# The modulation row moved from a TensorE stage at the start into VectorE's time inside the two feed-forwards

## The chip, the cores and the metric

The kernel runs on one core of a Trainium2 chip. The metric is the device time of one execution in microseconds (us), the median of several runs.

## The reference, cut to what matters

A stream `x` of 256 tokens by 1024 runs through two blocks in float32. The first has a retention mixer, a feed-forward, a gated linear recurrence and a second feed-forward. The second block scales and shifts its normed input by a modulation row, mixes with a context of 256 tokens, and ends in a product-key feed-forward. The modulation row depends on nothing that the first block computes:

```python
def swiglu_ffn(x, w_in, w_out):
    gate, up = jnp.split(x @ w_in, 2, axis=-1)
    return (jax.nn.silu(gate) * up) @ w_out
...
mod_l = jax.nn.silu(c) @ ada_w[i] + ada_b[i]          # c: (1, 1024), ada_w: (1024, 6144)
mod_c = jax.nn.silu(c_ctx) @ ada_w[i] + ada_b[i]
sh1, sc1, g1, sh2, sc2, g2 = jnp.split(mod_l[:, None, :], 6, axis=-1)
csh1, csc1, cg1, csh2, csc2, cg2 = jnp.split(mod_c, 6, axis=-1)
hl = rmsnorm(xl, norm1_g[i]) * (1.0 + sc1) + sh1
hc = rmsnorm(xc, norm1_g[i]) * (1.0 + csc1) + csh1
yc, yl = token_mixing(hc, hl, ...)
xl = xl + g1 * yl
hl2 = rmsnorm(xl, norm2_g[i]) * (1.0 + sc2) + sh2
xl = xl + g2 * peer_ffn(hl2, ...)
```

Of `mod_c` only the first two sixths (`csh1`, `csc1`) are used. `ada_w` is 25 MB.

## The kernel before, in words

Every large product is made of three TensorE products. A weight slot of 128 x 4096 float32 (2 MB; `wraw`, two buffers) is loaded by SyncE's queue, ScalarE copies it into a high part (`split_hi`, L934, four pieces), VectorE subtracts to get a low part (`split_lo`, L1300, four pieces), and TensorE multiplies high by high, low by high and high by low (`mm3`, L1831 to L1833). A slot's buffer is loaded again once VectorE has split it (`s_wlo`), and its split parts are overwritten once TensorE has used them (`s_wused`). PSUM banks 0 to 3 are handed round by `unit`, `take` and `free_bank`; banks 4 to 7 are an accumulator. Each engine runs its own program in a fixed order, written out by hand, and a waiting instruction holds all behind it on its engine.

**The start.** SyncE loads constants and the small parameter rows (`prow`), and then twelve slots of `ada_w`, with `x` after the fourth. TensorE turns the parameter rows into columns; ScalarE takes the silu of `c` and `c_ctx`, and through Abs, Exp and Ln (L974 to L978) with eleven small VectorE instructions (L1382 to L1394) makes a column that the recurrence needs. In `ada` each of the twelve slots is split and multiplied, 24 products of 512 columns a slot; VectorE adds the bias (L1403), and GpSimd stores 512 columns of the modulation row to DRAM (`mods`), from where they are later read back broadcast into `rows`. Then come norm 0 (squares L947, root L951, gain L1334, TensorE transposes L1893, high part L955, low part L1326), the retention input (twelve slots) and the retention heads. A head needs a masked score (L1433) ahead of its products with the values (L1971 to L1975).

**A feed-forward** has eleven "in" steps (a 2 MB slot; 96 products of 256 columns) and eleven "out" steps (a 1 MB slot; 24 products of 512 columns), in the order in 0, in 1, out 0, in 2, out 1, ..., in 10, out 9, out 10. In its step each engine splits the slot of the next step. After an "in" step VectorE multiplies gate by up (`ffn_hidden`, L1468) and GpSimd splits it (L813, L814). The middle sixteen steps are four trips of a hardware loop of four steps, with semaphore targets and addresses computed from the trip. During the second feed-forward the context is loaded, normed, modulated and transposed too (`norm_c`).

**The input of the recurrence** is a hardware loop of three trips; in each VectorE runs a four-tap convolution (L1488 to L1497) on one bank after another, every instruction waiting for the one before it.

## Time and profile before

| | |
|---|---|
| median of 3 runs | 2549.86 us (2546.12 to 2551.75) |
| the profiled execution, its own time | 2535.93 us |
| its span | 2534.1 us |
| TensorE matmul, busy | 2255.3 us (89%) |
| VectorE, busy | 1426.4 us (56%) |
| ScalarE, busy | 1061.1 us (42%) |
| GpSimd, busy | 294.2 us (12%) |
| read from HBM | 333.71 MB, 132 GB/s over the span |

In the rows below PE is TensorE's matmuls and PEld its weight loads, DVE VectorE, ACT ScalarE, POOL GpSimd, SPq SyncE's queue. L12 is line 12 of the kernel; many helpers are shared, so a line can serve several stages. The busy time of a stretch tells how full an engine was; the timeline's bracket tells how long the engine stood idle ahead of an instruction and what released it. "x4" merges instructions that follow each other, and their time is from the first start to the last end. A float32 product that is not split in parts shows as two matmul records.

### The profile page before, as it was taken

The page shows a single profiled execution, that of the slowest core. Times are in us where ns is not written, and L with a number is a line of the kernel's source. Part 1 is how long each engine was busy: PE and PEld are TensorE (multiplying, and loading weights), DVE is VectorE, ACT ScalarE, POOL GpSimd, SP SyncE. Part 2 cuts the span into 40 slices and gives each one's busy share as a digit, 9 for nine tenths or more (in the row PEclk, how much of TensorE's full clock was granted, in tenths as well). Part 3 has the DMA queues.
Part 4 walks back from the last instruction along what each step waited for, and adds up shares of the span by engine and source line. Part 5 has one row for each costly group of instructions (what it writes and reads, how often), then busy time and mean ns, then how long its engine had stood idle before and what let it go on. Part 6 is the DMA issues. An engine that isn't in the chain of part 4 may idle for free.

```text
span 2534.1 us, 38849 instructions
## 1 busy us (share of the span) xinstructions
PE 2255.3 (89%) x14663; PEld 2014.7 (80%) x14663; DVE 1426.4 (56%) x2220; ACT 1061.1 (42%) x1872; POOL 294.2 (12%) x307
## 2 busy tenths in 40 slices
PE   5799989979768997988998887989999999999997
PEld 4587678869758886977887467889999999877775
DVE  5753554466765455215445334699666663566665
ACT  4535343344553433313332243433444444555554
POOL 1120111111211120000003000000123342000000
PEclk9899999999879998988998588999999999999998
DMA  8845335453334445230010022334333334666664
GB/s 319 289 170 193 109 122 177 166 182 125 125 121 145 149 149 183 92 110 1 1 25 10 1 91 92 118 117 134 109 117 113 114 117 145 188 189 187 189 190 140
DMA packets 158604, 336.58 MB, mean 133 GB/s; under 512 B 17818, under 2 KB 69776, under 8 KB 158352
## 3 DMA queue, kind: packets, MB, share of 16 engines
q1 hardware_dynamic: 153872, 321.15, 39.4%
q0 software_dynamic: 4608, 13.68, 1.6%
q8 instruction: 88, 1.44, 0.2%
q14 instruction: 36, 0.29, 0.0%
HBM read 333.71 MB, written 1.10 MB: 132 GB/s over the span
## 4 chain that ended last, share of the span: by engine, by line
PE 54%; DVE 16%; PEld 15%; issue 5%; ACT 3%; DMA 3%; PEldq 2%; POOL 0%; SPq 0%; DVEq 0%; ACTq 0%
PE psum L1831 12%; PE psum L1833 12%; PE psum L1832 12%; PEld psum L1831 5%; PEld psum L1832 5%; PEld psum L1833 5%; DVE weights_lo L1300 5%; PE psum L2304 4%; PE psum L2351 2%; PEldq L1878 2%; ACT weights_hi L934 2%; PE psum L2168 2%; PE psum L2174 2%; DMA weights<-in_ada_w_dram 1%; DVE u_lo L1781 1%
## 5 line engine op out<-in xcount | busy, mean ns | idle before, releaser
L1300 DVE TENSOR_TENSOR weights_lo<-weights,weights_hi 128x1024 fp32r<-128x1024 f32 (+2 forms) x384 | 446.4, 1225 | 217.2 <-ACT weights_hi L934 215.7
L934 ACT ACTIVATE weights_hi<-weights 128x1024 fp32r<-128x1024 f32 (+2 forms) x384 | 335.0, 945 | 281.7 <-PEq L1878 161.6
L1831 PE MATMUL psum<-input_hi,weights_hi 128*128 128x256 f32 x1288 | 373.0, 290 | 46.4 <-DVE weights_lo L1300 32.4
L1832 PE MATMUL psum<-input_lo,weights_hi 128*128 128x256 f32 x1288 | 369.3, 287 | 0.0
L1833 PE MATMUL psum<-input_hi,weights_lo 128*128 128x256 f32 x1288 | 368.8, 286 | 0.0
L1831 PE MATMUL psum<-input_hi,u_hi 128*128 128x256 f32 x1024 | 301.5, 294 | 0.0
L1831 PEld LDWEIGHTS psum<-input_hi,weights_hi 128*128 128x128 f32 x1288 | 251.9, 196 | 58.2 <-issue 33.0
L1832 PE MATMUL psum<-input_lo,u_hi 128*128 128x256 f32 x1024 | 290.6, 284 | 0.0
L1833 PE MATMUL psum<-input_hi,u_lo 128*128 128x256 f32 x1024 | 290.5, 284 | 0.0
L1781 DVE TENSOR_TENSOR u_lo<-psum,u_hi 128x512 fp32r<-128x512 f32 x256 | 164.9, 685 | 178.5 <-ACT u_hi L1231 177.3
L1833 PEld LDWEIGHTS psum<-input_hi,weights_lo 128*128 128x128 f32 x1288 | 252.1, 196 | 0.0
L1832 PEld LDWEIGHTS psum<-input_lo,weights_hi 128*128 128x128 f32 x1288 | 252.0, 196 | 0.0
L1831 PE MATMUL psum<-v_hi,act_hi 128*128 128x512 f32 x512 | 203.4, 397 | 0.0
L1833 PE MATMUL psum<-v_hi,act_lo 128*128 128x512 f32 x512 | 200.4, 391 | 0.0
L1832 PE MATMUL psum<-v_lo,act_hi 128*128 128x512 f32 x512 | 200.0, 391 | 0.0
L1832 PEld LDWEIGHTS psum<-input_lo,u_hi 128*128 128x128 f32 x1024 | 197.6, 193 | 0.0
L1831 PEld LDWEIGHTS psum<-input_hi,u_hi 128*128 128x128 f32 x1024 | 197.0, 192 | 0.0
L1833 PEld LDWEIGHTS psum<-input_hi,u_lo 128*128 128x128 f32 x1024 | 196.9, 192 | 0.0
L1231 ACT ACTIVATE u_hi<-psum 128x512 fp32r<-128x512 f32 x256 | 139.4, 597 | 42.1 <-PE psum L2304 35.8
L2304 PE MATMUL psum<-ident,u_rows 128*128 128x128 f32 x1024 | 135.9, 276 | 17.4 <-DVE u_lo L1781 16.4
L2304 PEld LDWEIGHTS psum<-ident,u_rows 128*128 128x128 f32 x1024 | 116.1, 142 | 21.6 <-issue 19.8
L1808 DVE TENSOR_TENSOR act_lo<-act_table,act_hi 128x256 fp32r<-128x256 f32 x128 | 54.7, 428 | 136.9 <-ACT act_hi L1277 136.9
(367 smaller groups left out, 4217.8 us busy)
## 6 DMA issues: line engine op xcount, KB each, us to landing
u_rows<-in_peer_u_dram SPq DMA_DIRECT2D x128, 512.0 KB, 3.6
weights<-in_ffn_w_in_dram SPq DMA_DIRECT2D x44, 1024.0 KB, 6.5
v_rows_even<-in_peer_v_dram SPq DMA_DIRECT2D x64, 512.0 KB, 3.6
v_rows_odd<-in_peer_v_dram SPq DMA_DIRECT2D x64, 512.0 KB, 3.6
weights<-in_ada_w_dram SPq DMA_DIRECT2D x24, 1024.0 KB, 7.5
weights<-in_ret_w_in_dram SPq DMA_DIRECT2D x24, 1024.0 KB, 6.4
weights<-in_ffn_w_out_dram SPq DMA_DIRECT2D x44, 512.0 KB, 7.1
weights<-in_lru_w_in_dram SPq DMA_DIRECT2D x12, 1024.0 KB, 6.7
```

The lines of the kernel that those rows point to most:

```text
L934: nc.scalar.activation(whi[:, r, at_], wraw[:, r, at_], ACT.Copy).then_inc(s_whi[r], 1)
L1231: nc.scalar.activation(UTH[:, b, 4 * h:4 * h + 4, :], PS[:, h, :].rearrange("p (k e) -> p k e", k=4), ACT.Copy).then_inc(s_uh[b], 1)
L1300: ins = nc.vector.tensor_tensor(wlo[:, r, at_], wraw[:, r, at_], whi[:, r, at_].bitcast(F32), ALU.subtract)
L1781: nc.vector.tensor_tensor(UTL[:, b, 4 * h:4 * h + 4, :], PS[:, h, :].rearrange("p (k e) -> p k e", k=4), UTH[:, b, 4 * h:4 * h + 4, :].bit ...
L1808: nc.vector.tensor_tensor(AL[:, b:b + 1, :], GT[:, bass.ds(4 * i + j, 1), :], AH[:, b:b + 1, :].bitcast(F32), ALU.subtract).then_inc(s_as, 1)
L1831: nc.tensor.matmul(o, ah, bh, start=start, stop=False)
L1832: nc.tensor.matmul(o, ah, bl, start=False, stop=False)
L1833: return nc.tensor.matmul(o, al, bh, start=False, stop=stop)
L1878: pe.drain().then_inc(s_wused[r], 1)
L2168: ins = nc.tensor.matmul(quarter(j), AM[d][:, j // 2, j % 2, :], XX[d][:, j // 2, j % 2, :], start=True, stop=True)
L2174: ins = nc.tensor.matmul(quarter(j), TI[d][:, j // 2, j % 2, :], YY[d][:, j // 2, j % 2, :], start=True, stop=True)
L2304: ins = nc.tensor.transpose(PS[:, h, q * P:(q + 1) * P], UR[:, b, at_:at_ + P], ident[:, :])
```

## The change

The `ada` stage at the start goes. Its sum is made on VectorE as 128 fused multiply-adds of 128 x 512 (`ada_product`): each takes a block of 128 rows of `ada_w`, unsplit, times a column of silu(c) or silu(c_ctx), plus the running sum. Twelve blocks of 512 columns are made: 0 to 5 in the first feed-forward, 80 products, eight in each of steps 1, 3, ..., 19; 6 to 11 in the second, 48 products, six in each of steps 5, 7, ..., 19. They stand behind `split_lo` and ahead of the `ffn_hidden` product of an "in" step. In the step after a block's last product TensorE adds up the 128 partitions by a float32 product with a column block of ones (two products for blocks 0 to 3, one for the others), ScalarE copies the result and GpSimd stores it.

The 24 halves of `ada_w` (1 MB each) have two buffers of their own, `AW`, beside the feed-forward's. SyncE loads them between the feed-forward's slots, each behind a wait (`s_awused`) for the half that lay there before. The first two wait for the end of the mixer ahead (`s_acc`), whose tiles lie there. The bias is loaded into partition 0 of a zeroed tile.

At the start `x`, the identity and two retention slots are loaded first, the parameter rows next, and norm 0 comes first on all engines. The Abs, Exp, Ln chain and its VectorE instructions stand between the retention input and the heads. All hardware loops of these stages are written out. The readers of `mods` wait for the stores (`stored`). `IOTA` shares `prow`'s place.

```diff
+FFN_STEPS = [("in", 0)]
+for _n in range(FI - 1):
+    FFN_STEPS += [("in", _n + 1), ("out", _n)]
+FFN_STEPS += [("out", FI - 1)]
+ADA_SLOTS = {"ffn0": range(0, 6), "ffn1": range(6, 12)}
+ADA_FIRST = {"ffn0": 1, "ffn1": 5}
+ADA_STEP = {"ffn0": 8, "ffn1": 6}
+BOTH = 4
+def ada_products(name):
+    return [(q, k, m) for q in ADA_SLOTS[name] for k in range(KT) for m in range(2 if q < BOTH else 1)]
+def ada_step(name, n):
+    return ADA_FIRST[name] + 2 * (n // ADA_STEP[name])
+def ada_made(name, at_):
+    return [p for n, p in enumerate(ada_products(name)) if ada_step(name, n) == at_]
+def ada_summed(name, at_):
+    last = {p[0]: ada_step(name, n) for n, p in enumerate(ada_products(name))}
+    return [q for q in ADA_SLOTS[name] if last[q] + 1 == at_]
+def ada_loaded(name, at_):
+    halves = [(q, h) for q in ADA_SLOTS[name] for h in range(2)]
+    last = {(p[0], p[1] // 4): ada_step(name, n) for n, p in enumerate(ada_products(name))}
+    return [half for n, half in enumerate(halves)
+            if (ADA_LOAD[name] if n < 2 else last[halves[n - 2]] + 2) == at_]
+ADA_LOAD = {"ffn0": 1, "ffn1": 2}
...
 SyncE
-            ada(0)
-            sp.dma_start(X[:, :, :], ...).then_inc(s_xload, 16)
-            with sp.Fori(1, 3) as i:
-                ada(i)
+            sp.dma_start(X[:, :, :], ...).then_inc(s_xload, 16)
+            sp.dma_start(ident[:, :], cols("ident")).then_inc(s_ident, 16)
+            for j in range(2):
+                wide(SLOTS["ret_in"] + j, W["ret_w_in"], j * BANK)
...
+            def load_ada(q, h):
+                if 2 * q + h >= 2:
+                    sp.wait_ge(s_awused, 2 * q + h - 1)
+                if h == 0:
+                    sp.wait_ge(s_azero, 1)
+                    sp.dma_start(AB[0:1, q % 4, :], A["ada_b_2"][0:1, q * BANK:(q + 1) * BANK]).then_inc(s_ab[q % 4], 16)
+                sp.dma_start(AW[:, h, :, :], W["ada_w_2"][:, 4 * h:4 * h + 4, q * BANK:(q + 1) * BANK])\
+                    .then_inc(s_aw[h], 16)
...
+                def load_context(at_):
+                    if at_ == ADA_LOAD[name]:
+                        sp.wait_ge(s_acc, 2 if name == "ffn0" else 6)
+                    for q, h in ada_loaded(name, at_):
+                        load_ada(q, h)
+                    if name == "ffn1" and at_ == 2:
+                        sp.dma_start(XC[:, :, :], ...).then_inc(s_ctx, 16)
...
 GpSimd
+                    for q in ada_summed(name, at_):
+                        evacuated(ada_unit(q))
+                        for half in range(2 if q < BOTH else 1):
+                            pool.dma_start(mods[half:half + 1, q * BANK:(q + 1) * BANK],
+                                           astage[64 * half:64 * half + 1, q % 2, :]).then_inc(s_ast[q % 2], 16)
...
 ScalarE
-            rounds(act, 3, ada)
             norm(0)
+            split_hi(0)
...
+                    for q in ada_summed(name, at_):
+                        b = take(ada_unit(q))
...
+                        nc.scalar.activation(astage[rows_, q % 2, :], PS[rows_, b, :], ACT.Copy).then_inc(s_free[b], 1)
...
 VectorE
+            def ada_product(q, k, m):
+                if (k, m) == (0, 0):
+                    dve.wait_ge(s_csilu, 1)
+                    dve.wait_ge(s_ab[q % 4], 16 * (q // 4 + 1))
...
+                chain.done(nc.vector.scalar_tensor_tensor(
+                    total, AW[:, k // 4, k % 4, :], csilu[:, 8 * m + k:8 * m + k + 1],
+                    total if k else AB[:, q % 4, :], ALU.mult, ALU.add))
...
+                def step(kind, n, at_):
+                    split_lo(sbase + at_ + 1, n=after(at_, last))
+                    for q, k, m in ada_made(name, at_):
+                        ada_product(q, k, m)
                     if kind == "in":
...
 TensorE
-            rounds(pe, 3, ada)
+                    for q in ada_summed(name, at_):
+                        b = free_bank(ada_unit(q))
...
+                        pe.wait_ge(s_asum, q + 1)
+                        for m in range(2 if q < BOTH else 1):
+                            ins = nc.tensor.matmul(PS[64 * m:64 * m + 64, b, :], ones[:, :], AS[m][:, q % 2, :],
+                                                   start=True, stop=True)
```

## Rows read from the trace of the kernel before

**Rows 1.** Busy time by stretch: start:end, length, each engine's time (instructions), TensorE clock, DMA share, GB/s

```profile
0.00:115.60 115.60, 75.66 (x289) 57.13 (x289) 74.03 (x85) 59.27 (x66) 20.07 (x44) 0.96 0.90 317
346.00:551.00 205.00, 186.77 (x1296) 171.56 (x1296) 99.88 (x95) 70.07 (x96) 34.08 (x22) 1.00 0.46 154
```

**Rows 2.** Chain of waits that ended last, first 130 us: start, length, what

```profile
51.22 11.05 DMA weights<-in_ada_w_dram
...
120.77 0.38 PE psum L1831
```

**Rows 3.** Busy time of two short stretches of the start, same columns as the first group

```profile
2.00:4.00 2.00, 0.00 (x0) 0.00 (x0) 0.00 (x0) 0.03 (x1) 2.00 (x4) 1.00 0.47 179
14.00:17.00 3.00, 0.00 (x0) 0.00 (x0) 1.13 (x7) 0.00 (x0) 0.00 (x0) 1.00 1.05 389
```

**Rows 4.** Timeline, first norm: start, length, engine, line, out<-in, count, idle before and its releaser

```profile
111.25 1.04 ACT L947 ACTIVATE normed<-residual 128x1024 f32<-128x1024 f32 x1
...
119.02 0.60 ACT L955 ACTIVATE input_hi<-psum 128x512 fp32r<-128x512 f32 x1 [0.26 <-PE psum L1893]
...
120.67 4.63 DVE L1300 TENSOR_TENSOR weights_lo<-weights,weights_hi 128x1024 fp32r<-128x1024 f32 x4 [0.32 <-ACT weights_hi L934]
```

**Rows 5.** Timeline, all engines, first 30 us

```profile
9.77 0.20 ACT L974 ACTIVATE small<-param_cols 128x12 f32<-128x12 f32 x1
...
15.16 0.17 DVE L1394 TENSOR_SCALAR small<-small 128x12 f32<-128x12 f32 x1
...
26.36 0.63 PE L1832 MATMUL psum<-weights_lo,c_hi 128*128 128x512 f32 x1
...
28.23 0.39 PE L1832 MATMUL psum<-weights_lo,c_hi 128*128 128x512 f32 x1
```

**Rows 6.** Timeline, all engines, one pair of feed-forward steps

```profile
408.90 0.69 DVE L1468 TENSOR_TENSOR ffn_hidden<-psum,ffn_gate 128x512 f32<-128x512 f32 x1 [9.55 <-PE psum L1833]
...
410.01 8.77 DVE L1300 TENSOR_TENSOR weights_lo<-weights,weights_hi 128x1024 fp32r<-128x1024 f32 x8 [0.42 <-ACT weights_hi L934]
...
410.87 2.15 POOL L814 TENSOR_TENSOR ffn_lo<-ffn_hidden,ffn_hi 128x512 fp32r<-128x512 f32 x1
...
414.96 2.19 ACT L934 ACTIVATE weights_hi<-weights 128x512 fp32r<-128x512 f32 x4 [2.13 <-PE psum L1833]
...
416.51 0.38 PE L1831 MATMUL psum<-input_hi,weights_hi 128*128 128x256 f32 x1 [1.65 <-DVE weights_lo L1300]
416.54 1.01 SPq L686 DMA_DIRECT2D weights<-in_ffn_w_in_dram  x2
...
418.95 0.89 SPq L686 DMA_DIRECT2D weights<-in_ffn_w_out_dram  x2
...
428.40 0.69 DVE L1468 TENSOR_TENSOR ffn_hidden<-psum,ffn_gate 128x512 f32<-128x512 f32 x1 [9.62 <-PE psum L1833]
```

**Rows 7.** Groups of instructions, VectorE, whole span, shapes apart: count, busy, mean ns, idle before

```profile
L1497 DVE SCALAR_TENSOR_TENSOR lru_u<-lru_padded,param_cols,lru_u 128x256 f32 x36 | 17.4, 485 | 5.4 <-DVE lru_u L1497 1.8 <-DVE lru_u L1495 1.8
...
L1512 DVE SCALAR_TENSOR_TENSOR lru_q<-lru_q,lru_r 128x512 f32<-128x512 f32 x6 | 4.2, 692 | 0.2
```

**Rows 8.** DMA to landing of the weight loads issued at 416.5 and at 419

```profile
DMA to landing us min/median/max: 5.2/6.4/7.6
...
DMA to landing us min/median/max: 7.1/7.4/7.8
```

**Rows 9.** Timeline, VectorE, first trip of the recurrent block's input loop

```profile
590.77 0.41 DVE L1495 TENSOR_SCALAR lru_u<-lru_padded,param_cols 128x256 f32 x1 [0.44 <-DVE lru_padded L1488]
...
593.43 0.41 DVE L1495 TENSOR_SCALAR lru_u<-lru_padded,param_cols 128x256 f32 x1 [0.32 <-DVE lru_u L1497]
...
603.51 10.77 DVE L1300 TENSOR_TENSOR weights_lo<-weights,weights_hi 128x1024 fp32r<-128x1024 f32 x8 [0.53 <-DVE lru_u L1497]
```

**Rows 10.** Timeline, ScalarE and VectorE, first retention head

```profile
262.50 0.60 ACT L998 ACTIVATE gate_silu<-psum 128x512 f32 x1 [4.84 <-PE psum L1833]
...
264.44 0.56 DVE L1433 TENSOR_TENSOR scores<-psum,decay 128x384 f32<-128x384 f32 x1 [7.16 <-PE psum L1961]
```

**Rows 11.** Chain of waits that ended last, retention heads

```profile
266.58 0.86 PE psum L1974 x2
```

**Rows 12.** Timeline, ScalarE and TensorE, end of the first feed-forward

```profile
551.08 3.90 ACT L934 ACTIVATE weights_hi<-weights 128x1024 fp32r<-128x1024 f32 x4 [3.72 <-PE psum L1833]
...
551.28 0.47 PE L1831 MATMUL psum<-weights_hi,ffn_hi 128*128 128x512 f32 x1 [0.30 <-PE psum L1833]
```

More of the change, by code:

```diff
@@ L191, in slot, with ffn_steps, ffn_unit, ada_unit @@
     return s0 % 2, i * (per // 2) + s0 // 2
-FFN_HEAD = [("in", 0), ("in", 1), ("out", 0)]
-FFN_BODY = [("in", 2), ("out", 1), ("in", 3), ("out", 2)]
-FFN_TAIL = [("in", FI - 1), ("out", FI - 2), ("out", FI - 1)]
-FFN_TRIPS = (FI - 3) // 2
-FFN_BASE = {"ffn0": 0, "ffn1": FI}
-FFN_SIZE = {"in": SLOT, "out": 2 * D}
-def ffn_steps(eng, base, step, chain=None, per=0, early=None, late=None):
-    for k, (kind, n) in enumerate(FFN_HEAD):
-        step(kind, n, base + k)
-    if early:
-        early()
-    with eng.Fori(0, FFN_TRIPS) as i:
-        if chain:
-            chain.enter(i, per)
-        for k, (kind, n) in enumerate(FFN_BODY):
-            step(kind, n, base + len(FFN_HEAD) + k, i)
-    if chain:
-        chain.leave(FFN_TRIPS)
-    if late:
-        late()
-    for k, (kind, n) in enumerate(FFN_TAIL):
-        step(kind, n, base + 2 * FI - len(FFN_TAIL) + k)
-def rounds(eng, trips, body):
-    body(0)
-    with eng.Fori(1, trips) as i:
-        body(i)
-def ffn_unit(name, n):
-    return UNITS[name] + 2 * n + (4 if name == "ffn1" and n >= 2 else 0)
-def after(base, s0, last):
-    order = FFN_HEAD + FFN_BODY * FFN_TRIPS + FFN_TAIL
-    n = s0 - base + 1
-    return FFN_SIZE[order[n][0]] if n < len(order) else last
+def ffn_steps(step, beside=None):
+    for at_, (kind, n) in enumerate(FFN_STEPS):
+        step(kind, n, at_)
+        if beside:
+            beside(at_)
+def ffn_unit(name, n, half=0):
+    return UNITS[name] + FFN_UNITS[name].index(("in", 2 * n + half))
+def ada_unit(q):
+    name = "ffn0" if q in ADA_SLOTS["ffn0"] else "ffn1"
+    return UNITS[name] + FFN_UNITS[name].index(("ada", q))
+def after(at_, last):
+    return FFN_SIZE[FFN_STEPS[at_ + 1][0]] if at_ + 1 < len(FFN_STEPS) else last
 NA_STEPS = TT * 8
@@ L422, in first_and_second_block @@
         split_at = stage.at
+        beside_ffn = Region("beside the feed-forward", stage_at + 16 * KB, split_at - stage_at - 16 * KB)
+        AW = beside_ffn.take("ada_rows_in", [P, 2, 4, BANK])
+        AS = [beside_ffn.take("ada_sums", [P, 2, BANK]),
+              Region("context, before it", split_at, 4 * KB).take("ada_sums_c", [P, 2, BANK])]
+        astage = beside_ffn.take("ada_rows", [P, 2, BANK])
         CH = stage.take("context_hi", [P, KT, S], F32R)
@@ L501, in first_and_second_block @@
         HKT = low.take("picks_t", [P, 3, S])
-        IOTA = low.take("iota", [P, P])
+        IOTA = prow
         GE = low.take("gates", [P, 2, 4, P])
@@ L1036, in _ @@
             norm(2)
-            with act.Fori(0, 3) as i:
+            for i in range(3):
                 for j in range(2):
@@ L1369, in _ @@
             nc.vector.memset(eps_col, EPS).then_inc(s_eps, 1)
+            nc.vector.memset(ones[:, :], 1.0).then_inc(s_ones, 1)
+            norm(0)
+            split_lo(0)
             b = take(UNITS["param"])
@@ L1471, in step, with beside @@
                         dve.sem_inc(s_free[b], 1)
[L1473 removed]
+                def beside(at_):
+                    if name == "ffn1" and at_ == 2:
+                        modulated("norm_c", XC, CH, CL)
+                ffn_steps(step, beside)
             norm(1)
@@ L1479, in _ @@
             chain.done(nc.vector.memset(UP[:, :, 0:3], 0.0))
-            with dve.Fori(0, 3) as i:
-                chain.enter(i, 2 * 9)
+            for i in range(3):
                 for j in range(2):
@@ L1500, in _ @@
                         dve.sem_inc(s_uc, 1)
-            chain.leave(3)
             split_lo(SLOTS["lru_gate"] + 1, n=3072)
@@ L1944, in _ @@
                     used(r)
-            with pe.Fori(0, 4) as i:
+            for i in range(4):
                 for j in range(2):
@@ L2015, in _ @@
             transposes(2)
-            with pe.Fori(0, 3) as i:
+            for i in range(3):
                 for j in range(2):
```

281 lines of the change are left out of this document (133 added, 148 removed).

## The prediction

> **What bounds the kernel now.** I read the busy times by stretch first. The first 115.6 us are a stage that DMA sets: the 16 DMA engines are busy 0.90 of it at 317 GB/s, while TensorE is busy 75.66 us [rows 1]. The chain of waits says the same: its long links there are weight slots of the modulation matrix on their way, one of 11.05 us, and the retention input's first product starts only at 120.77 us [rows 2]. The feed-forwards are another kind of stage: in 346 to 551 us TensorE is busy 186.77 of 205 us, VectorE only 99.88 us, and DMA 0.46 of its time [rows 1]. So I read the timeline of one pair of steps there, to see where VectorE, SyncE's queue and DMA have room and which wait ends last. The pair's period is 428.40 - 408.90 = 19.5 us [rows 6]. The chain in it is: "in" products end, ScalarE's first high piece, four low pieces on VectorE, next "in" products. TensorE does the "out" step meanwhile and then stands for 1.65 us, until VectorE's low parts at 416.51 [rows 6].
>
> **The front.** The 25 MB leave the start. What then sets the first retention product? `x` (1.05 MB) shares DMA with GpSimd's three gain rows (1.57 MB). Traffic is at 179 GB/s in 2 to 4 us and at 389 GB/s once full [rows 3]; half filled, 2.1 MB take some 6 us from 2.5 us on, so I put `x` at 8.5 us (estimate; 6 to 11 as bounds). From the first square (111.25) to the end of ScalarE's last high copy (119.02 + 0.60) are 8.4 us, then ScalarE turns to the slot's high parts: 16.9 us, plus 1 us for transposes on a slow TensorE, 17.9. The low parts start 1.05 us after such a turn (120.67 against 119.62) and take 4.63 us [rows 4]. That gives 23.6 us. The data come sooner: `x`, gain rows, identity and the first slot are 4.8 MB, 12.4 us at 389 GB/s from some 3.5 us on; the parameter rows, which TensorE now waits for behind both slots, are at 6.9 MB, some 22 us. I take 23.6 where 120.77 stood: **-97.2 us**. Here the old stage hid a cost: its first matmuls took 0.63 us each and those after 27.2 us 0.39 us [rows 5], 4 us at about half speed under a DMA wait. Now that falls on the retention input, which TensorE sets: half of 4 us, **+2**. The twelve slots of 2.1 MB need 5.4 us each at 389 GB/s and TensorE takes some 12, so DMA doesn't bind there.
>
> **The heads.** The Abs to last small VectorE instruction took 9.77 to 15.33 us, 5.6 us, with two table loads inside [rows 5]. At the start it hid behind the first slot's loading. Its new place is behind the last gate copy, which ends at 262.50 + 0.60 = 263.10; so it ends at 268.7, and VectorE's first masked score, at 264.44 before, is queued behind it [rows 10]: 4.3 us. TensorE's products with the values wait for that score. After such a pause it may be slow again for a few products; nothing shows it here, 0 to 2 us, and I take 0.7 because the float32 products there are short: **+5**.
>
> **The recurrence's input.** Written out, the loop loses its computed targets and addresses. In a trip VectorE stands 0.44 and 0.32 us ahead of each first tap, both kinds twice, and 0.53 ahead of the next split [rows 9], 2.05 us; where nothing new is computed the same wait for the instruction before is 5.4/36 = 0.15 us [rows 7]. Five times 0.15 are 0.75, so 1.3 us a trip could go, and VectorE is in the chain there: three trips, 3.9. I take **-3.7**; bounds 0 and -5.
>
> **The products inside the feed-forwards.** A product is 692 ns, a fused multiply-add of the same 128 x 512, plus 0.15 us for its wait: 0.85 us, eight are 6.8 us [rows 7]. VectorE has finished both splits at 410.01 + 8.77 = 418.78, so products end at 425.6, and the gate product comes at 428.40 when TensorE is done [rows 6]. 2.8 us are left, and they cover the work entirely. If the cover went, each microsecond past 428.4 would cost one in each of the 18 pairs with products. All 128 products are 109 us of VectorE, at nothing on the path. In a pair that ends a block ScalarE's high parts of the "out" slot (414.96) now queue behind TensorE's one or two products with ones and a copy of 0.6 us. A float32 product of 512 columns is 0.86 us [rows 11], so two and the copy push those high parts 2.5 us and the low parts, which had slack in front of them, some 1.8; products then end at 427.4, still ahead.
>
> TensorE: two products are 1.7 us in a gap of 1.65 and start a little late, 0.3 us for each of blocks 0 to 3, and nothing for the eight with one product: +1.2. At the end of each feed-forward there's no gap: out 10 follows out 9 by 0.30 us at 551.28, and ScalarE's next high parts at 551.08 lie on the chain into the norm [rows 12]. One product, the copy and their hand-overs stand ahead, 1.8 us, twice: +3.6. The trips' boundaries and computed waits go: the pairs should lose 0.1 us, sixteen of them, -1.6 (bounds 0 and -4). Sum **+3.2**.
>
> SyncE's queue is the tight place. A load of the next half waits there for the half's products, at 425.6, and behind it waits the "out" slot, which was issued at 418.95. Together they are 2 MB, like the "in" pair, whose last landed 7.6 us after its own issue, half a microsecond behind the first [rows 6, 8]: some 8 us. So the "out" slot lands at 433.6 where ScalarE wants it at 414.96 + 19.5 = 434.5. It is a loop of its own: landing 8, first high piece 0.6, low parts 2.7, products 6.8, hand-overs 0.3, together 18.4 against 19.5. After a block's end it is late by about 1 us, which the 2.8 us take up. The "in" slot is issued before the wait, at 416.54, and isn't touched. GpSimd's stores, half a microsecond each to issue, fall where it idles, and the readers of the row come far later.
>
> VectorE and GpSimd: the eight splits take 8.77 us where alone they'd be 4.63 + 2.7; the surplus falls beside GpSimd's work of 410.87 to 413.02 [rows 4, 6]. The products run at 418.8 to 425.6, clear of it. The Trainium skill (GPSIMD Engine Reference, Specifications) says that GpSimd's SBUF interface is shared with VectorE, with contention when a VectorE instruction has two SBUF inputs, as each of these products has. The splits beside GpSimd agree. By that rule the products would be slowed if the two met; on this timetable they don't, and the sum would be the same.
>
> **Sum.** -97.2 + 2 + 5 - 3.7 + 3.2 = -90.7, on the profiled execution's 2535.9: 2445. The runs' median is 2549.86, 14 us above that execution; I carry the difference over: 2549.9 - 90.7 = **2459 us**.
>
> **Rivals.**
> - *SyncE's loop binds.* If half and "out" slot land after 11 us, not 8 (one slot of the first stage took 11.05 [rows 2]), the loop is 21.4 us and some 18 pairs lose 1.9 each: +34, 2493. Against it: DMA here is busy under half the time. Chance 0.15.
> - *Products meet GpSimd.* The splits went from 7.3 to 8.8 us beside 2 to 3 us of its work [rows 6], a slowdown of 1.3 if all is charged to four splits of 4.63. Eight products at 1.3 times 0.85 are 8.9 us and end at 427.7, still covered; but the loop is 20.5, 1.0 over, in the ten pairs of the first feed-forward (six products stay under in the second): +10, 2469. The skill's rule named above speaks for it, the order in time against. Chance 0.06.
> - *The front comes later.* `x` at 11 us, a cold TensorE through both the transposes and the first slot, parameter rows that arrive last: +8, 2467. Nothing in the old trace shows `x` alone. Chance 0.14.
> - *More is gained*: written-out waits save 0.3 us a pair and `x` lands at 6: -8, 2451. Chance 0.07.
> - *Slower than before.* One mechanism: the "out" slot, held in SyncE's queue behind `s_awused`, comes so late that it drags every pair. It decides from 4.5 us a pair, 91/20, so at a landing of some 14 us instead of 8; at 15 the loop is 25.4 us and costs 5.9 in 20 pairs, 118, which gives 2577. Nothing shows such a landing for 2 MB at half load. Chance 0.02.
> - *It doesn't do what it says*: the start stays as long, because loads of the retention slots take the matrix's place as the bound, 2550. They'd have to come at under a third of the measured rate. Chance 0.01.
>
> The likeliest holds 0.55. What a measurement here can't tell from no change is about 0.2%, 5 us.
>
> **Range and chances.** The likeliest, the late front, the larger gain and the products beside GpSimd hold 0.82 and lie at 2451 to 2469; with 8 us below and 13 above for their own bounds (the loops' 0 instead of -3.7, the pause's 2 us, the spread of 6 us among three runs) I take 2443 to 2482. Faster 0.97, same 0.01, slower 0.02.
>
> **What would show it.** The first retention product at 22 to 26 us, and its first ones at half speed. The first masked score 5.6 us behind the last gate copy. Feed-forward pairs of 19.4 to 19.8 us, VectorE's products between 418.8 and 425.6 of such a pair with over 2 us idle behind them, each 0.69 us and 0.85 apart. The "out" slot's high parts still released by TensorE and not by a DMA. Wrong if the high parts wait for the "out" slot's DMA, if the gate product waits for the products, or if the front ends past 32 us.

## The result, and the profile after

The kernel after takes **2436.6 us** (median of 6 runs, 2411.5 to 2441.8) where the one before takes 2550.2 (6 runs, 2546.1 to 2556.4): ratio 0.9552, 95% interval 0.951 to 0.9594. The forecast was 2459 us in 2443 to 2482. The sign was right and the gain bigger: 113.6 us between the medians, 90.7 forecast, and the time lies 6.4 us below the range. The profiled execution of after took 2429.3 us with a span of 2427.5, 106.6 under that of before.

To see where they went I cut both traces at the same marks, VectorE's products of `ffn_hidden` (L1468 before, L1521 after; eleven in each feed-forward). Lengths in us:

| | before | after | difference | forecast |
|---|---|---|---|---|
| start to the first product of feed-forward 0 | 358.02 | 264.58 | -93.4 | -90.2 |
| first to last product of feed-forward 0 | 187.03 | 185.39 | -1.6 | +0.4 |
| its last product to the first of feed-forward 1 | 219.77 | 212.67 | **-7.1** | -1.9 |
| first to last product of feed-forward 1 | 199.93 | 196.03 | **-3.9** | -0.8 |
| its last product to the end | 1569.35 | 1568.83 | -0.5 | +1.8 |

(The forecast's terms laid on these stretches: -97.2 + 2 + 5; +1.2 of the products with ones and half of the -1.6; +1.8 - 3.7; the other half of the -1.6; +1.8. A feed-forward's stretch holds one step of 12.0 us and nine pairs.) The stretches in bold are those that came out too well. Each length is from one execution; the same stretch of kernels that don't differ in it moves by some 2 to 3 us from one execution to the next (the front of before 357.9 to 360.4, the third stretch of after 211.1 to 213.5), so single differences of 1 or 2 us say little.

**The front.** Timeline of after, all engines, the rows that answer to [rows 4]: start, length, engine, line, out<-in, count, idle before and what ended it.

```profile
6.01 1.28 ACT L994 ACT_TABLE_LOAD   x1 [6.01 <-DMA residual<-in_x_dram]
...
16.26 3.90 ACT L981 ACTIVATE weights_hi<-weights 128x1024 fp32r<-128x1024 f32 x4 [0.22 <-DMA weights<-in_ret_w_in_dram]
17.34 4.63 DVE L1350 TENSOR_TENSOR weights_lo<-weights,weights_hi 128x1024 fp32r<-128x1024 f32 x4 [0.58 <-ACT weights_hi L981]
...
23.50 0.43 PE L1974 MATMUL psum<-ident,param_rows 118*128 118x118 f32 x1 [8.09 <-DMA param_rows<-in_sc_conv_w_dram]
23.63 0.55 PE L1880 MATMUL psum<-input_hi,weights_hi 128*128 128x256 f32 x1
...
28.67 0.41 PE L1882 MATMUL psum<-input_hi,weights_lo 128*128 128x256 f32 x1
...
29.68 0.28 PE L1882 MATMUL psum<-input_hi,weights_lo 128*128 128x256 f32 x1
```

The first retention product stands at 23.63, the forecast to 0.03 us, but not by the forecast's chain: the low parts are done at 17.34 + 4.63 = 21.97, 1.6 us sooner than I had them, and the parameter rows, put at "some 22", end TensorE's wait at 23.50. That the two errors meet so closely is luck. `x` was there at 6.01, not at 8.5. The products take 0.41 us until 29.1 and 0.28 from then on.

**The heads.** Timeline of after, the rows that answer to [rows 10].

```profile
165.21 0.60 ACT L1031 ACTIVATE gate_silu<-psum 128x512 f32<-128x512 f32 x1 [4.84 <-PE psum L1882]
...
165.93 1.28 ACT L1035 ACT_TABLE_LOAD   x1
...
171.11 0.17 DVE L1460 TENSOR_SCALAR small<-small 128x12 f32<-128x12 f32 x1
171.19 1.01 DVE L1465 TENSOR_TENSOR scores<-psum,decay 128x384 f32<-128x384 f32 x2
171.99 1.37 PE L2007 MATMUL psum<-values,scores 128*128 128x512 f32 x2 [3.70 <-DVE scores L1465]
```

The first masked score is 5.4 us behind the last gate copy (171.19 - 165.81), and TensorE stood 3.70 us for it. Busy time by stretch after that pause (start:end, length, each engine's time, TensorE clock, DMA share, GB/s) shows a mean granted clock of 0.67 of the full 2.4 GHz, so a part of it at the lower level, 1.2 GHz:

```profile
171.90:177.00 5.10, 5.01 (x10) 2.42 (x11) 1.64 (x4) 0.00 (x0) 0.00 (x0) 0.67 0.00 0
```

**A pair of feed-forward steps.** Timeline of after, answering to [rows 6].

```profile
315.12 0.69 DVE L1521 TENSOR_TENSOR ffn_hidden<-psum,ffn_gate 128x512 f32<-128x512 f32 x1 [2.10 <-PE psum L1882]
316.61 8.32 DVE L1350 TENSOR_TENSOR weights_lo<-weights,weights_hi 128x1024 fp32r<-128x1024 f32 x8 [0.79 <-ACT weights_hi L981]
321.44 2.19 ACT L981 ACTIVATE weights_hi<-weights 128x512 fp32r<-128x512 f32 x4 [2.02 <-DMA weights<-in_ffn_w_out_dram]
322.58 0.39 PE L1880 MATMUL psum<-input_hi,weights_hi 128*128 128x256 f32 x1 [1.52 <-DVE weights_lo L1350]
324.86 0.74 DVE L1498 SCALAR_TENSOR_TENSOR ada_sums<-ada_rows_in,small,ada_sums 128x512 f32<-128x512 f32 x1
...
330.35 0.75 DVE L1498 SCALAR_TENSOR_TENSOR ada_sums_c<-ada_rows_in,small,ada_sums_c 128x512 f32<-128x512 f32 x1
331.19 0.37 SPq L712 DMA_DIRECT2D ada_rows_in<-in_ada_w_dram  x1
331.60 0.98 SPq L726 DMA_DIRECT2D weights<-in_ffn_w_out_dram  x2
334.38 0.69 DVE L1521 TENSOR_TENSOR ffn_hidden<-psum,ffn_gate 128x512 f32<-128x512 f32 x1 [3.27 <-PE psum L1882]
```

The pair is 19.26 us long, and all nine of the first feed-forward are 19.26 or 19.27. The eight products start 0.785 us apart ((330.35 - 324.86) / 7), end at 331.1, and 3.27 us are left behind them; in pairs that end a block 2.10 (the first row). One thing that I had named as a sign of a wrong forecast is there: in this pair the high parts of the "out" slot wait for its DMA, 2.02 us. VectorE's eight splits run through without a gap all the same, so nobody waits for them.

DMA issues of the next half and "out" slot (KB each, median us from issue to landing):

```profile
ada_rows_in<-in_ada_w_dram SPq DMA_DIRECT2D x1, 1024.0 KB, 5.3
weights<-in_ffn_w_out_dram SPq DMA_DIRECT2D x2, 512.0 KB, 6.5
```

**The recurrence's input.** Timeline of after, VectorE and then ScalarE, one trip of what was the loop, answering to [rows 9].

```profile
497.00 0.41 DVE L1550 TENSOR_SCALAR lru_u<-lru_padded,param_cols 128x256 f32<-128x256 f32 x1 [0.16 <-DVE lru_padded L1543]
497.44 1.53 DVE L1552 SCALAR_TENSOR_TENSOR lru_u<-lru_padded,param_cols,lru_u 128x256 f32<-128x256 f32 x3
...
502.01 3.90 ACT L981 ACTIVATE weights_hi<-weights 128x1024 fp32r<-128x1024 f32 x4 [7.73 <-PEq L1927]
...
526.02 3.90 ACT L981 ACTIVATE weights_hi<-weights 128x1024 fp32r<-128x1024 f32 x4 [7.72 <-PEq L1927]
```

From one trip's high parts to the next one's are 526.02 - 502.01 = 24.01 us. Before, ScalarE's rows for the same places are these (timeline, ScalarE):

```profile
595.48 1.28 ACT L934 ACT_TABLE_LOAD   x1 [7.60 <-PEq L1878]
596.78 3.90 ACT L934 ACTIVATE weights_hi<-weights 128x1024 fp32r<-128x1024 f32 x4
602.21 1.28 ACT L1043 ACT_TABLE_LOAD   x1 [1.53 <-PE psum L1833]
...
624.47 3.90 ACT L934 ACTIVATE weights_hi<-weights 128x1024 fp32r<-128x1024 f32 x4
```

There it was 624.47 - 596.78 = 27.69 us: 3.7 us more a trip, where I had costed 1.3. (The loop has two such full turns; behind its last copy of a bank VectorE saves 2.3 us more.) Two things differ. In the loop ScalarE loads its activation table twice in each trip, which I had not looked at, and VectorE waits ahead of each instruction. The Trainium skill (ScalarE activation tables: per-element evaluation and per-set limits, Table sets in the compiler and the runtime) says that the back end places the table loads per block. A loop's body that is such a block would load at each trip, as this one does, 1.28 us each.

**The end of a feed-forward.** Timeline of after, ScalarE, answering to [rows 12].

```profile
457.28 0.59 ACT L1074 ACTIVATE ada_rows<-psum 64x512 f32<-64x512 f32 x1 [5.01 <-PE psum L2054]
457.77 3.89 ACT L981 ACTIVATE weights_hi<-weights 128x1024 fp32r<-128x1024 f32 x4
461.57 1.01 ACT L994 ACTIVATE normed<-psum 128x1024 f32<-128x1024 f32 x1
```

The squares that open the norm start 461.57 - 449.97 = 11.60 us behind the last `ffn_hidden` product. Before (timeline, ScalarE) they stood 554.89 - 545.05 = 9.84 us behind it, with no copy ahead of the high parts, so the tail costs 1.76 us:

```profile
554.89 1.01 ACT L947 ACTIVATE normed<-psum 128x1024 f32<-128x1024 f32 x1
```

### The profile page after: what moved, and what is told of

Its sections match the earlier page's. It is cut to its first block, busy times and chain, and to the rows that moved or that the text cites. A ratio compares the mean times of both kernels' runs of the same rounds, so it can differ in the third digit from the quotient of the medians.

```text
span 2427.5 us, 37415 instructions
## 1 busy us (share of the span) xinstructions
PE 2189.9 (90%) x14407; PEld 1960.1 (81%) x14407; DVE 1453.3 (60%) x2285; ACT 1000.8 (41%) x1821; POOL 287.2 (12%) x288
## 4 chain that ended last, share of the span: by engine, by line
PE 57%; DVE 17%; PEld 16%; ACT 3%; PEldq 2%; issue 2%; DMA 1%; SPq 1%; POOL 0%; DVEq 0%; ACTq 0%
PE psum L1880 13%; PE psum L1881 13%; PE psum L1882 13%; DVE weights_lo L1350 6%; PEld psum L1880 5%; PEld psum L1881 5%; PEld psum L1882 5%; PE psum L2352 4%; PE psum L2399 2%; PEldq L1927 2%; PE psum L2216 2%; PE psum L2222 2%; ACT weights_hi L981 1%; DVE u_lo L1830 1%; PE psum L2197 1%
## 5 line engine op out<-in xcount | busy, mean ns | idle before, releaser
L1350 DVE TENSOR_TENSOR weights_lo<-weights,weights_hi 128x1024 fp32r<-128x1024 f32 (+2 forms) x336 | 390.2, 1223 | 212.9 <-ACT weights_hi L981 211.3
L981 ACT ACTIVATE weights_hi<-weights 128x1024 fp32r<-128x1024 f32 (+2 forms) x336 | 288.0, 931 | 233.1 <-PEq L1927 175.8
```

The costliest lines, as they stand in the source:

```text
L981: nc.scalar.activation(whi[:, r, at_], wraw[:, r, at_], ACT.Copy).then_inc(s_whi[r], 1)
L1350: ins = nc.vector.tensor_tensor(wlo[:, r, at_], wraw[:, r, at_], whi[:, r, at_].bitcast(F32), ALU.subtract)
```

## Experiments

Each run of after's kind is compared by the marks of the table above, and by its time where it was timed.

### Which part of the gain is the move, which the written-out loops

Three kernels: before with all these loops written out (ScalarE's, VectorE's, TensorE's, SyncE's and GpSimd's of the retention input, feed-forwards and recurrence input), before with those of the recurrence input alone, and after with those of the recurrence input put back.

```diff
 before, feed-forwards (the other two alike)
-    with eng.Fori(0, FFN_TRIPS) as i:
-        if chain:
-            chain.enter(i, per)
+    for i in range(FFN_TRIPS):
         for k, (kind, n) in enumerate(FFN_BODY):
-            step(kind, n, base + len(FFN_HEAD) + k, i)
-    if chain:
-        chain.leave(FFN_TRIPS)
+            step(kind, n + 2 * i, base + len(FFN_HEAD) + k + 4 * i)
```

> The kernel before, with the hardware loops of the retention input, the feed-forwards and the recurrence's input written out, and the modulation stage left where it was. Theory A (what the prediction under-sized is the written-out loops, not the move): the profiled span falls by 14 to 18 us, of which about 2 in the first feed-forward, 7 between the two feed-forwards and 5 in the second, where no pair is 20.9 us any more; ratio to before about 0.994. Theory B (the loops are worth what I predicted, 5.3 us, and the move itself gave the rest): 4 to 6 us.

> The kernel before with only the three-trip loop of the recurrence's input written out. Theory A: a trip falls from 27.6 to about 24.0 us, because a table load of 1.28 us in front of ScalarE's high parts goes in each trip besides VectorE's computed waits; from the end of the first feed-forward to the start of the second 8 to 9 us less. Rival (only the computed waits count): 3.7 us.

> The changed kernel with that one loop turned back into a hardware loop. Theory A: 8 to 9 us slower than the changed kernel between the feed-forwards, all else as it was, with two table loads in each trip again. Rival (the stretch is shorter because the modulation rows or the start shifted something): no more than 4.

| us | to the first product | feed-forward 0 | between | feed-forward 1 | rest | median, ratio to before |
|---|---|---|---|---|---|---|
| before | 358.02 | 187.03 | 219.77 | 199.93 | 1569.35 | 2548.8 (19 runs) |
| all written out | 357.49 | 185.40 | 208.07 | 194.96 | 1577.58 | 2525.3 (10), 0.9906 [0.9866, 0.9945] |
| recurrence's written out | 360.23 | 187.02 | 209.93 | 201.37 | 1577.75 | 2538.4 (10), 0.9961 [0.9918, 1.0005] |
| after, recurrence's put back | 264.29 | 185.43 | 221.14 | 195.29 | 1581.25 | 2449.8 (4), 0.9618 [0.9546, 0.969] |

The first four stretches sum to 964.75 us before and to 945.92 with all loops written out: **18.8 us** for the loops, 11.7 of them in the stretch with the recurrence's input. I had -5.3 for them. The last column is a measurement of its own, 23.5 us between the medians (ratio's interval 0.55 to 1.34%, 14 to 34 us). From there to after it is 945.92 - 858.67 = 87.3 us for the move itself, where the forecast's terms up to this mark, -97.2 + 2 + 5 + 1.2 + 1.8, give 87.2. In the sum the move was sized right, and what failed is the price of a loop. But that the two figures meet within 0.1 us is luck: against the kernel with all loops written out, the front gave 92.9 us where the terms say 90.2, and the stretch between the feed-forwards lost 4.6 (212.67 - 208.07) where they say 1.8. Of these 4.6 the tail explains 1.8; the rest, 2.8 us here and 1.3 by the second profile of after below, no run accounts for. Putting one loop back costs 8.5 us in its stretch (221.14 - 212.67; 10.0 against the second profile of after), writing it out saves 9.8. That run's own ratio includes 1, so its whole time shows nothing; the stretch does.

A part of the second feed-forward's gain has another face. Before, timeline of TensorE and busy time by stretch around one of its two pairs of 20.92 us:

```profile
852.45 0.39 PE L1831 MATMUL psum<-input_hi,weights_hi 128*128 128x256 f32 x1 [1.78 <-DVE weights_lo L1300]
```

```profile
852.40:854.00 1.60, 1.55 (x10) 1.55 (x11) 1.60 (x3) 0.56 (x2) 0.00 (x0) 0.81 0.25 22
854.00:856.00 2.00, 2.00 (x12) 2.00 (x11) 0.81 (x2) 0.00 (x0) 0.00 (x0) 0.50 0.93 306
856.00:858.00 2.00, 2.00 (x16) 2.00 (x15) 0.00 (x0) 0.00 (x0) 0.00 (x0) 0.80 1.10 360
```

Behind this pause of 1.78 us the granted clock falls to 0.50, the lower of the two levels, and the pair is 1.3 us longer than its neighbours of 19.60. But four pairs later, in the same execution, a pause of the same length leaves the clock at 1.00 (the same two views):

```profile
933.49 0.39 PE L1831 MATMUL psum<-input_hi,weights_hi 128*128 128x256 f32 x1 [1.78 <-DVE weights_lo L1300]
```

```profile
934.00:936.00 2.00, 2.00 (x19) 2.00 (x19) 1.84 (x4) 0.00 (x0) 0.00 (x0) 1.00 0.63 162
```

So the length of the pause alone doesn't decide it. In all three kernels that kept the feed-forwards' loops on the base of before, three pairs of the second one are 20.9 to 21.1 us long, behind pauses of 1.75 to 1.78; with the loops written out and single products these pairs have pauses of 1.5 to 1.6 us at most and none is that long. Written out, the pauses are shorter and the clock stayed up; that the one causes the other is argued, not shown.

### Whose loop it was: table loads or computed waits

```diff
 ScalarE alone
-            with act.Fori(0, 3) as i:
+            for i in range(3):
                 for j in range(2):
                     split_hi(SLOTS["lru_in"] + j + 1, i, 2)
 VectorE alone
-            with dve.Fori(0, 3) as i:
-                chain.enter(i, 2 * 9)
+            for i in range(3):
...
-            chain.leave(3)
```

> The kernel before with only ScalarE's loop of three trips in the recurrence's input written out; TensorE's, VectorE's and SyncE's stay loops. All four written out took the stretch between the feed-forwards from 219.8 to 209.9 us. Theory A (ScalarE's two table loads a trip, 1.28 us each, lie on the chain in front of the high parts and of the copy that frees TensorE's bank): nearly all of it goes, the trip falls from 27.65 us to 24.0 to 25, the stretch to 210 to 212. Theory B (the computed waits of VectorE's convolution set the trip): VectorE's 13.87 us from the first copy to the next low parts stay, a trip loses at most 1 us, the stretch is 217 to 220 us, though the table loads are gone.

> The kernel before with only VectorE's loop of three trips in the recurrence's input written out; ScalarE keeps its loop and its two table loads a trip. Theory B (VectorE's computed waits set the trip: its stretch from the first copy of a bank to the next low parts is 13.87 us in the loop and 11.27 us written out, 2.6 us a trip): the trip falls to some 25 us and the stretch between the feed-forwards from 219.8 to some 212 us. Theory A (the table loads do): VectorE is done sooner and waits for ScalarE's high parts or TensorE, the trip stays over 27 us and the stretch is 217 to 220 us.

Timeline with ScalarE's loop alone written out, VectorE's rows:

```profile
593.26 0.69 DVE L1488 COPY lru_padded<-psum 128x512 f32<-128x512 f32 x1
...
607.11 10.77 DVE L1300 TENSOR_TENSOR weights_lo<-weights,weights_hi 128x1024 fp32r<-128x1024 f32 x8 [0.53 <-DVE lru_u L1497]
619.46 0.69 DVE L1488 COPY lru_padded<-psum 128x512 f32<-128x512 f32 x1 [1.58 <-PE psum L1833]
```

and with VectorE's alone:

```profile
590.73 0.69 DVE L1487 COPY lru_padded<-psum 128x512 f32<-128x512 f32 x1
...
592.03 1.52 DVE L1496 SCALAR_TENSOR_TENSOR lru_u<-lru_padded,param_cols,lru_u 128x256 f32<-128x256 f32 x3
...
601.97 6.61 DVE L1300 TENSOR_TENSOR weights_lo<-weights,weights_hi 128x1024 fp32r<-128x1024 f32 x4
610.65 4.63 DVE L1300 TENSOR_TENSOR weights_lo<-weights,weights_hi 128x1024 fp32r<-128x1024 f32 x4 [2.06 <-ACT weights_hi L934]
615.24 0.69 DVE L1487 COPY lru_padded<-psum 128x512 f32<-128x512 f32 x1
```

The stretch between the feed-forwards is 219.20 us with ScalarE's loop gone and 212.28 with VectorE's (219.77 before, 209.93 with the loop gone from all four engines). The one run of each took 2519.5 and 2545.0 us beside 2545.3 of before; the part behind the last feed-forward, which neither touches, was 1549.7 and 1584.7 us, so the whole times say nothing here. VectorE's loop, with its computed waits and its own turns, is the larger part, 7.5 of 9.8 us. From the copy to the next low parts VectorE takes 601.97 - 590.73 = 11.24 us instead of 603.51 - 589.64 = 13.87 (the copy before starts at 589.64). The reason is in the rows: I had taken 0.15 us as what a wait for the instruction before costs in any case, since [rows 7] shows 5.4 us for 36 of them. That was the price in a loop. With constant waits the three fused instructions of a tap chain take 1.53 us together, so some 0.04 lies between two of 0.485, where in the loop each pair had 0.15 between. Writing out ScalarE's loop alone, and with it the table loads, took 1.5 us off the first turn (619.46 - 593.26 = 26.20) and nothing off the second, which stays 27.64 us by VectorE's copies as before; the stretch is 0.6 shorter. 1.1 us is lost ahead of the loop (its first high parts stand 40.0 us behind the last product of feed-forward 0, 38.9 before), and I did not follow that up. With VectorE's loop alone written out the turns take 24.5 us, with all four 24.0: beside it ScalarE's loop and its table loads are worth 0.5 us a trip.

### Are the products free, and what is SyncE's queue worth

Four kernels on the base of after: a quarter of the products (those of blocks 0 and 4 of each sum only), every product made twice, and the loads of the matrix's halves put behind the "out" slot in SyncE's queue, that alone and together with the doubled products. The first leaves out three quarters of the modulation row's sum, the doubled ones add each product twice.

```diff
 a quarter
-                chain.done(nc.vector.scalar_tensor_tensor(
+                if k % 4 == 0:
+                    chain.done(nc.vector.scalar_tensor_tensor(
 twice
+                for twice in range(2):
...
-                        total if k else AB[:, q % 4, :], ALU.mult, ALU.add))
+                        total if k or twice else AB[:, q % 4, :], ALU.mult, ALU.add))
 behind the "out" slot
-            if (ADA_LOAD[name] if n < 2 else last[halves[n - 2]] + 2) == at_]
+            if (ADA_LOAD[name] if n < 2 else last[halves[n - 2]] + 3) == at_]
```

> The changed kernel with 32 of the 128 multiply-adds (the first of each four, so the modulation row is not the reference's); loads, waits and TensorE's sums stay. If the products are wholly covered, the pairs stay 19.27 us and the total is the changed kernel's within 1 us. If they cost anything, through VectorE or through SyncE's wait for them, the pairs get shorter: by 0.3 us or more each, 5 us or more in all.

> The changed kernel with every multiply-add done twice in a row (so the modulation row is not the reference's): sixteen at 0.785 us are 12.6 us in a pair of the first feed-forward, twelve are 9.4 us in one of the second. Theory 'VectorE's cover decides' (6.3 us of products and 2.1 to 3.3 us of idle time behind them): pairs of about 22.3 to 23.5 us in the first, and the 19.3 us of now in the second, whose 9.4 us just fit. Theory 'SyncE's loop decides' (landing 8, high piece 0.6, low parts 2.7, products, hand-overs 0.5): 24.4 us in the first and 21.2 us in the second.

> The changed kernel with each half's load issued behind the 'out' slot of the next step and not ahead of it, so that SyncE's wait for the products no longer holds the 'out' slot. If the wait is covered as it stands, nothing changes: pairs of 19.27 us, total within 1 us; the 'out' slot's high parts are then released by TensorE with several us to spare. If it costs, the pairs get shorter.

> The doubled products (not the reference's row) together with the halves issued behind the 'out' slot. 'VectorE's cover decides': no change against the doubled products alone. 'SyncE's loop decides': the first feed-forward's pairs fall from 24.4 to about 22.3 to 23.5 us, the second's from 21.2 to about 19.3.

| us | a pair of feed-forward 0 | feed-forward 0 | feed-forward 1 | median |
|---|---|---|---|---|
| after | 19.26 | 185.39 | 196.03 | 2436.6 (6) |
| a quarter | 19.25 to 19.27 | 185.39 | 195.69 | 2443.9 (4) |
| twice | 23.3 to 24.0 | 230.91 | 202.07 | 2469.9 (1) |
| behind | 19.26 | 185.38 | 195.19 | 2445.5 (1) |
| twice and behind | 22.5 to 23.1 | 222.35 | 199.69 | 2484.5 (1) |

With 96 of the 128 products gone not one pair is shorter: they cost nothing. Doubled, they add 6.28 us to a pair that has 3.27 or 2.10 to cover them, so 3.0 or 4.2 should show, some 3.6 in the mean. The timeline with the products made twice:

```profile
353.24 0.69 DVE L1522 TENSOR_TENSOR ffn_hidden<-psum,ffn_gate 128x512 f32<-128x512 f32 x1 [0.36 <-DVE ada_sums_c L1499]
354.09 6.55 DVE L1350 TENSOR_TENSOR weights_lo<-weights,weights_hi 128x1024 fp32r<-128x1024 f32 x4 [0.15 <-DVE ffn_hidden L1522]
...
384.39 2.19 ACT L981 ACTIVATE weights_hi<-weights 128x512 fp32r<-128x512 f32 x4 [7.88 <-DMA weights<-in_ffn_w_out_dram]
```

The gate product now waits for VectorE's own products, and the "out" slot's high parts 7.9 us for their DMA. With the halves behind that slot in the queue the nine pairs grow by 3.45 us in the mean (22.71 - 19.26), as the cover says; without, by 4.4 (23.66 - 19.26). So VectorE's time sets the pair first, and SyncE's held queue adds 0.95 us to it. In the second feed-forward, where I had expected the doubled products to fit, they cost 6.0 us (202.07 - 196.03), and 3.7 with the halves behind. With single products the order in the queue changes nothing: 19.26 either way, and with the halves behind, the "out" slot's high parts at 321.13 are again released by TensorE and not by the DMA.

One place has hardly any cover: the first step, a single "in" step of 12.0 us that holds eight products too. In after (timeline, VectorE) the gate product waits there only 0.57 us, and with the products made twice that step takes 17.96 us.

```profile
276.59 0.69 DVE L1521 TENSOR_TENSOR ffn_hidden<-psum,ffn_gate 128x512 f32<-128x512 f32 x1 [0.57 <-PE psum L1882]
```

The rival "SyncE's loop binds" is there as a mechanism, and a price of it was seen only past the point where VectorE binds too.

### The column between input and heads, and the last copy

Two kernels on after: the Abs, Exp, Ln column made beside the retention input (ScalarE's part ahead of its part 1, VectorE's behind the ninth of its low parts), and with that ScalarE's last copy of each feed-forward behind the high parts that open the norm. Beside the second, after itself once more.

```diff
 ScalarE, step 21 of a feed-forward
-                    for q in ada_summed(name, at_):
+                    for q in ada_summed(name, 20 if at_ == 21 else 99 if at_ == 20 else at_):
```

> The changed kernel with the Abs, Exp, Ln chain and its small VectorE instructions moved from the front of the heads into the retention input, between its value part and its gate part, where VectorE and ScalarE are idle over 5 us in each slot. If the chain costs what the prediction says, the heads start 4 to 5 us sooner, and with no pause of 3.7 us TensorE's first products with the values aren't slow: 5 to 6.5 us in all by the first gate product of the feed-forward. Rival (it costs the same wherever it stands, since the splits behind it are late): 0 to 1 us.

> The kernel after, with two of its costs moved off the path. The Abs, Exp, Ln column stands earlier, as in the run with the column alone, and ScalarE makes its last copy of each feed-forward's modulation row behind the high parts that open the next norm instead of ahead of them. Theory (the column lies on the path and costs 6.05 us; the copy, which waited 5.01 us for TensorE's product with ones at 457.28, holds up the high parts and squares that open the norm): the first product of the first feed-forward stands at 258.5 instead of 264.58, and the squares of the next norm start 9.9 us behind the last hidden product instead of 11.6, so 1.7 us less behind each feed-forward. Together 6.0 + 3.4 = 9.4 us under the kernel after. Rival (the squares wait for TensorE's transposes or for the weights anyway): the column's 6 us alone, and the stretch between the feed-forwards stays at 212.7 us.

> The kernel after once more, unchanged, beside the others on one chip: it shows by how much the time behind the last feed-forward, which no edit touches, moves the sum from one execution to the next. Theory (that time was 1562.7 to 1587.3 us in the profiles so far, with the granted clock): first product of the first feed-forward at 264.6, its ten pairs 185.4 us, the stretch to the second 212.7, the second 196.0, and all that differs from the first profile, up to 20 us, lies behind it. Rival (the spread comes from the front or the feed-forwards): these four differ by more than a microsecond each.

| us | to the first product | feed-forward 0 | between | feed-forward 1 | rest | median |
|---|---|---|---|---|---|---|
| after | 264.58 | 185.39 | 212.67 | 196.03 | 1568.83 | 2436.6 (6) |
| after again | 265.07 | 185.40 | 211.12 | 195.17 | 1588.04 | 2435.1 (6) |
| column early | 258.53 | 185.41 | 212.63 | 195.99 | 1583.24 | 2437.6 (1) |
| column early, copy late | 259.08 | 185.40 | 210.63 | 195.25 | 1580.84 | 2435.6 (6) |

The column cost 6.0 us where it stood, in both pairs of kernels, 1 more than the +5 forecast. Timeline with the copy late, ScalarE:

```profile
450.50 3.90 ACT L981 ACTIVATE weights_hi<-weights 128x1024 fp32r<-128x1024 f32 x4 [3.72 <-PE psum L1883]
454.31 0.57 ACT L1074 ACTIVATE ada_rows<-psum 64x512 f32<-64x512 f32 x1
454.79 1.01 ACT L994 ACTIVATE normed<-psum 128x1024 f32<-128x1024 f32 x1
```

The squares stand 454.79 - 444.48 = 10.31 us behind the last `ffn_hidden` product (it starts at 444.48) instead of 11.60: 1.3 us won; the stretch between is 0.5 to 2.0 us shorter. The first four stretches sum to 850.36 us, 6.4 and 8.3 under the two profiles of after, and yet the medians of six runs on one chip are 2435.6 and 2435.1. This is no version that can be called faster than after: 6 to 8 us disappear in what follows, in runs that spread over 34 us and more.

"After again" shows where that spread is here: its first four stretches are 856.76 us, 1.9 under the first profile, its last one 19.2 over. Busy time of 100 us of it, from 500 us behind the last `ffn_hidden` product, in after:

```profile
1358.67:1458.67 100.00, 76.67 (x449) 64.47 (x447) 45.76 (x54) 39.99 (x60) 2.16 (x4) 0.86 0.34 116
```

and in after again:

```profile
1356.76:1456.76 100.00, 77.86 (x296) 60.18 (x295) 41.23 (x50) 33.34 (x51) 2.16 (x4) 0.64 0.25 87
...
1375.00:1400.00 25.00, 24.12 (x84) 18.16 (x83) 4.08 (x9) 6.57 (x14) 0.00 (x0) 0.50 0.00 0
```

The same kernel gets TensorE at 0.86 in the one and at 0.64 in the other, over 25 us at 1.2 GHz with TensorE busy 24.12, and does 449 products in one and 296 in the other.

## Why the prediction was right and wrong

- **The front, -97.2: right** (-97.14 between the first retention products), by a chain that had two errors of opposite sign, the low parts 1.6 us sooner and the parameter rows 1.5 us later than put. What bound at the end was the DMA of the rows, so the figure's closeness is luck.
- **The cold clock, +2:** 5.5 us at 0.21 between starts instead of 0.12, 2.4 us, is there. But the stretch as a whole is no longer than before: from the first retention product to the last gate copy 141.58 us against 141.73.
- **The heads, +5:** 6.0 by the run without it. Up to the score they are 4.0 (5.4 us behind the gate copy, 1.3 before), forecast 4.3; the other 2 I put down to TensorE at a mean clock of 0.67 after its pause of 3.70 us, where I had put 0.7. Yet this term and the last were +7 together, and from the first retention product to the first product of feed-forward 0 after is only 3.7 us longer (240.95 against 237.25). Some 2 us were gained in the heads or behind them that no run accounts for.
- **The written-out loops, -3.7 and -1.6: the step that failed.** They were put at 5.3 us in all and are worth 18.8 in the profiles, so the mechanism was there and its price was wrong. In the recurrence's input the term was sized by [rows 9] and [rows 7], five long waits at 2.05 us of which 0.75 stay: 1.3 us a trip. Measured, 3.7 for each full turn: VectorE saves 2.6 between the copy and the low parts, since the short waits between the taps go too, which the forecast took to stay at 0.15. ScalarE's two table loads of 1.28 us a trip, which it left out, are worth 0.5 beside that. That loop alone is 9.8 us in its stretch, against 3.7. In the feed-forwards the forecast had 0.1 for each of sixteen pairs, 1.6 us; the first one alone gave 1.6 (0.2 a pair), the second 5.0, 2.6 of it as two pairs with a fallen clock.
- **The products, 0: right.** 0.75 us each and 0.785 apart instead of 0.69 and 0.85; eight take 6.28 instead of 6.8, and the cover left is 3.27, not 2.8. Leaving out three quarters of them changes no pair. What the forecast overlooked is that one of its "18 pairs" is the single first step, where 0.57 us of cover is left.
- **SyncE's loop: the time right, the sign for it wrong.** The half and the slot land 5.3 and 6.5 us behind their issues where I had 8 for both, and yet ScalarE's high parts wait for the slot in some pairs. The wait ends before anyone needs them.
- **The ones' products in the gap, +1.2: not there.** Pairs with two, one and none are 19.26 or 19.27. **The tails, +1.8 each: right.** The squares stand 11.60 us behind the last product against 9.84, and 1.3 of that comes back with the copy late.
- **The rival "more is gained"** (chance 0.07) had the direction and two of the signs, `x` at 6 us and shorter pairs. But the early `x` bought nothing, since the rows' DMA bound, and the loop that gave most wasn't in it.
- **The total.** Of the 22.6 us between 2459.2 and 2436.6, 13.5 are the loops (18.8 - 5.3), some 2 are in the stretch behind, and the move's own errors cancel. The other 7 come from carrying the 14 us by which before's profiled execution lay under its median over to after, whose profiled execution lies 7.3 under its own. With the loops sized right the forecast would have been 2445.5, still 8.9 above the measured median.

## What to carry to other kernels

When a change writes a hardware loop out, price the loop by comparing a trip with what its instructions take and with a written-out neighbour: look for the gap between dependent instructions, which is itself a cost of computed waits, and for table loads inside the body. Work moved under a busier engine was free here up to the idle time measured ahead of the next instruction that waits, and cost about one for one past it. Look for the step with the least of that idle time, not the typical one. Where an untouched block's time varies by 20 us from run to run, compare stretch by stretch; six runs' medians didn't show 6 to 8 us here. And a sum that comes out to 0.1 us can hide errors of 3 us of either sign.

## What the runs showed of the hardware

- A hardware loop's body on ScalarE began each trip with a table load of 1.28 us, and had a second in it; written out, one load served all three trips.
- A VectorE instruction waiting for the one before it starts 0.15 us behind it when the wait is computed, and some 0.04 when it is constant (three of 0.485 in 1.53).
- A fused multiply-add of 128 x 512 with both tensors in SBUF takes 0.75 us here, where the one that I took its price from had 0.69 [rows 7].
- Four splits beside GpSimd's two instructions of 1.04 and 2.16 us take 6.2 us (6.6 in the recurrence's input) where alone they take 4.63. The products, which run clear of GpSimd, keep their 0.75. The Trainium skill (GPSIMD Engine Reference, Specifications) says that GpSimd shares its SBUF interfaces with VectorE, with contention for VectorE's instructions with two SBUF inputs; these splits fit that.
- TensorE's granted clock went to 0.50 behind two pauses of 1.78 us in the second feed-forward, stayed at 1.00 behind a third of 1.78, and stayed there behind the pauses of 1.52 of the kernels with the loops written out. In one stretch of an unchanged block it differed between two executions of one kernel, 0.86 and 0.64.
